# Retention on one core: weight sums by adding DMA transfers, sums of x kept in PSUM, scores between the third and the fourth quarter product

## What is computed

```python
def _retention(h, w_in, gn_g, w_out):            # h: normalised x, 512 x 1024
    proj = h @ w_in
    q, k, v, g = split(proj)                     # 4 heads, 256 wide for q and k, 512 for v and g
    q, k = _rope(q, pos), _rope(k, pos) * RET_DK ** -0.5
    ...                                          # over all chunks this is, per head:
    #   o[n] = sum over m of decay[n, m] * (q[n] . k[m]) * v[m]
    o = (o - mean(o)) * rsqrt(var(o) + EPS) * gn_g
    y = silu(g) * o
    return y @ w_out                             # added to x
```

## Time and profile before

| | us |
|---|---|
| median of 3 executions | 1906.8 (1903.63 to 1907.77) |
| the profiled execution, own time | 1903.31 |
| its span, first to last instruction | 1901.5 |
| busy in the span: PE, PEld | 1830.7 (96%), 1557.2 (82%) |
| busy in the span: DVE, POOL, ACT | 1262.2 (66%), 1018.6 (54%), 874.0 (46%) |

### The profile page before, as it was taken

The page is one execution under the profiler, slowest core; times in us unless marked ns, Lnnn a source line. Parts: engine busy times, 40 slices in busy tenths (PEclk is TensorE's granted clock), DMA queues, the critical chain, the costliest instruction groups (busy, mean ns, idle before and its releaser), DMA issues.

```text
span 1901.5 us, 23957 instructions
## 1 busy us (share of the span) xinstructions
PE 1830.7 (96%) x9348; PEld 1557.2 (82%) x9348; DVE 1262.2 (66%) x1908; ACT 874.0 (46%) x1350; POOL 1018.6 (54%) x431
## 2 busy tenths in 40 slices
PE   9999999999977999999899999999999999999998
PEld 7778889898865787878689898988888887888886
DVE  6986875776779667575766354457777766454546
ACT  5345443343543424243446444454666655453444
POOL 5573465475535365656438475665333335664755
PEclk9999999999997999999999999999999999999999
DMA  5222414423245325151342422312433223414221
GB/s 183 89 89 77 145 67 148 159 92 106 80 147 183 133 71 187 66 171 67 110 145 77 133 89 89 134 45 66 121 109 101 88 69 109 155 47 149 92 90 55
DMA packets 143344, 206.02 MB, mean 108 GB/s; under 512 B 4320, under 2 KB 94704, under 8 KB 142720
## 3 DMA queue, kind: packets, MB, share of 16 engines
q1 hardware_dynamic: 135968, 192.16, 30.2%
q10 hardware_dynamic: 7264, 12.34, 2.2%
HBM read 193.96 MB, written 10.53 MB: 108 GB/s over the span
## 4 chain that ended last, share of the span: by engine, by line
PE 72%; DVE 15%; ACT 4%; issue 3%; POOL 1%; DMA 0%; ACTq 0%; DVEq 0%
PE ps L858 23%; PE ps L860 23%; PE ps L859 23%; DVE ps L2315 1%; POOL w_lo L824 1%; ACT w_hi L1411 1%; DVE w_lo L2563 1%; DVE work L2611 1%; DVE raw L2549 1%; DVE diagonals L1983 1%; DVE work L2778 1%; DVE work L2574 0%; DVE probs_t_lo L2797 0%; PE ps L1198 0%; DVE x L2627 0%
## 5 line engine op out<-in xcount | busy, mean ns | idle before, releaser
L824 POOL TENSOR_TENSOR w_lo<-raw,w_hi 128x1024 fp32r<-128x1024 f32 x216 | 527.4, 2451 | 609.4 <-ACT w_hi L1411 609.4
L858 PE MATMUL ps<-xh,w_hi 128*128 128x512 f32 x1280 | 504.9, 394 | 4.6 <-DVE xl L2009 2.3
L860 PE MATMUL ps<-xh,w_lo 128*128 128x512 f32 x1280 | 498.9, 390 | 0.0
L859 PE MATMUL ps<-xl,w_hi 128*128 128x512 f32 x1280 | 498.8, 390 | 0.0
L1411 ACT ACTIVATE w_hi<-raw 128x1024 fp32r<-128x1024 f32 x242 | 252.2, 1057 | 392.9 <-PE ps L860 344.2
L858 PEld LDWEIGHTS ps<-xh,w_hi 128*128 128x128 f32 x1280 | 240.7, 188 | 58.5 <-issue 8.9
L859 PEld LDWEIGHTS ps<-xl,w_hi 128*128 128x128 f32 x1280 | 240.8, 188 | 50.7 <-issue 1.9
L860 PEld LDWEIGHTS ps<-xh,w_lo 128*128 128x128 f32 x1280 | 240.7, 188 | 50.7
L858 PE MATMUL ps<-hid,w_hi 128*128 128x256 f32 (+1 forms) x688 | 228.4, 332 | 2.1 <-DVE att_v L2751 1.1
L860 PE MATMUL ps<-hid,w_lo 128*128 128x256 f32 (+1 forms) x688 | 227.1, 330 | 0.0
L859 PE MATMUL ps<-hid,w_hi 128*128 128x256 f32 (+1 forms) x688 | 227.0, 330 | 0.0
(11 more groups left out here) (302 smaller groups left out, 3546.7 us busy)
## 6 DMA issues: line engine op xcount, KB each, us to landing
raw<-in_mlp_w_dram SPq DMA_DIRECT2D x40, 1024.0 KB, 5.5
work<-in_mlp_w_dram SPq DMA_DIRECT2D x16, 1024.0 KB, 5.5
raw<-in_ret_w_in_dram SPq DMA_DIRECT2D x12, 1024.0 KB, 5.2
raw<-in_att_w_in_dram SPq DMA_DIRECT2D x12, 1024.0 KB, 5.3
raw<-in_w_gate_dram SPq DMA_DIRECT2D x11, 1024.0 KB, 5.4
raw<-in_w_up_dram SPq DMA_DIRECT2D x11, 1024.0 KB, 5.5
hid<-position_sums SPq DMA_DIRECT2D x10, 1024.0 KB, 5.2
raw<-in_w_in_dram SPq DMA_DIRECT2D x9, 1024.0 KB, 5.1
```

Source lines behind the costliest of these rows:

```text
L824: nc.gpsimd.tensor_tensor(half_of(wl[:, b % 2, :], b, half), half_of(source, b, half), half_of(wh[:, b % 2, :], b, half).bitcast(F32), ALU ...
L858: nc.tensor.matmul(o, a[0], b[0], start=first, stop=False, skip_group_check=True)
L859: nc.tensor.matmul(o, a[0], b[1], start=False, stop=False, skip_group_check=True)
L860: return nc.tensor.matmul(o, a[1], b[0], start=False, stop=last, skip_group_check=True)
```

## The change

The signs of the seven products are changed so that each weight sum is one addition to a block already held: p1 = b12 + b11, p2 = p1 + b22, p3 = b22 + b12, p4 = p2 + b21. GpSimd issues each as a DMA transfer from DRAM that adds to the holder; no engine computes them, and the low halves of d2 and d4 go to GpSimd. The sums of x are formed in PSUM banks 6 and 7, in the order w (not stored), d2, d1, h22, d3; h22's stays in its place, so three are stored in place of four. `spread` moves behind h11, the scores of every head between h22 and d2, the mix of head 3 takes the order of the others. The normalising is folded into the gate: ScalarE scales the gate by the norm factor (`scale_gate`) and `gated` subtracts the mean and multiplies in one operation. The scaling of x (`scale_x`) moves to two later places of head 0. The core of the diff:

```diff
-BY_VECTOR = ("t2", "t4", "d2", "d4")
+BY_VECTOR = ("t2", "t4")
-        SUM_ROW = {"d1": 0, "d2": 1, "d3": 2, "h22": 3}
+        SUM_ROW = {"d1": 0, "d2": 1, "h22": 2, "d3": 3}
+        sum_rows = [o_sb[:, 2:4, :], ps[:, 6:8, :], o_sb[:, 0:2, :], ps[:, 6:8, :]]
+        root_guess = ps[:, 5, 0:ST]
+        sums_upto = {"w": 4, "d2": 8, "d1": 12, "h22": 16, "d3": 20}
...
 # SyncE
-                    fetch("b11", 0)
                     fetch("b12", 0)
+                    fetch("b22", 0)
...
                             converted("o0", h - 1)
-                            fetch("b22", h)
+                            fetch("b11", h)
                             converted("o1", h - 1)
                             fetch("b21", h)
+                        if more:
+                            converted("h11", h)
+                            fetch("q", h + 1)
                         multiplied("d1", h)
                         fetch_sum("d3")
                         if more:
-                            sp.wait_ge(d2_made, 2 * (h + 1))
-                            sp.wait_ge(d3_made, 2 * (h + 1))
-                            converted("h22", h)
-                            fetch("q", h + 1)
-                            multiplied("h22", h)
-                            fetch_sum("h22")
                             converted("d3", h)
                             fetch("k", h + 1)
...
 # GpSimd
+            def add_to(held, name, h, signal):
+                dst = holders[holder_of(held, h)].rearrange("p (k c) -> p k c", c=512)
+                nc.gpsimd.dma_start(dst, head_weights(name, h), accum_op=ALU.add).then_inc(signal, 16)
...
-                if kind == "h11":
-                    ...
-                        nc.gpsimd.tensor_tensor(first[:, cut], second[:, cut], first[:, cut], ALU.subtract).then_inc(d1_made, 1)
+                if kind == "own" and own_at[b][0] == "k":
+                    h = own_at[b][1]
+                    pool.wait_ge(*landed("b12", h))
+                    add_to("b12", "b11", h, p1_landed)
+                if kind == "d1":
+                    pool.wait_ge(w_lo, lows[2 * b + 2])
+                    add_to("b12", "b22", head_of(b), p2_landed)
                 if kind == "h22":
-                    ...
+                    pool.wait_ge(w_lo, lows[2 * b + 2])
+                    add_to("b22", "b12", head_of(b), p3_landed)
+                if kind == "d2":
+                    pool.wait_ge(w_lo, lows[2 * b + 2])
+                    add_to("b12", "b21", head_of(b), p4_landed)
...
 # TensorE
-                    spread()
                     for h in range(RET_HEADS):
                         head_quarter("h11", h)
+                        if h == 0:
+                            spread()
+                        head_quarter("d1", h)
+                        head_quarter("h22", h)
                         head_scores()
-                        for kind in ("d1", "h22", "d2", "d3"):
-                            head_quarter(kind, h)
+                        head_quarter("d2", h)
+                        head_quarter("d3", h)
                         pe.wait_ge(pt_ready, c.next(pt_ready, 4))
                         head_mix(h, (0, 1))
-                        if not more:
-                            head_mix(h, (2, 3))
                         head_quarter("h21", h)
-                        if more:
-                            head_mix(h, (2, 3))
+                        head_mix(h, (2, 3))
                         head_quarter("d4", h)
...
 # ScalarE
-                        act.wait_ge({"d1": d1_made, "d2": d2_made, "d3": d3_made, "d4": d4_made}[kind], 2 * h + half + 1)
+                        act.wait_ge({"d1": p1_landed, "d2": p2_landed, "d3": p3_landed, "d4": p4_landed}[kind], 16 * (h + 1))
...
+                    def scale_gate(h):
+                        act.wait_ge(root_refined, h + 2)
+                        for s in range(ST):
+                            act.wait_ge(gate_made, 4 * h + s + 1)
+                            nc.scalar.activation(sg[:, s, :], sg[:, s, :], ACT.Copy, scale=t4[:, s:s + 1]).then_inc(gate_scaled, c.made(gate_scaled))
...
                     def head(h, prepare=None):
+                        for _ in range(6):
+                            after_unit()
+                        scores_hi(range(ST))
                         after_unit()
                         after_unit()
-                        scores_hi((0, 1))
-                        after_unit()
-                        after_unit()
-                        scores_hi((2, 3))
-                        for _ in range(4):
-                            after_unit()
                         value_tile_hi(h, 0)
...
                         gate_curve(h, 2)
                         gate_curve(h, 3)
+                        scale_gate(h)
...
                     make_root()
+                    scale_far(4)
+                    position_sum_hi("d1")
+                    position_sum_hi("d2")
+                    qk_hi_of(qh)
+                    position_sum_hi("h22")
+                    act.wait_ge(sum_lo, SUM_ROW["d2"] + 1)
+                    scale_far(0)
+                    position_sum_hi("d3")
+                    make_root()
                     qk_hi_of(kh)
...
 # VectorE
-                        V.tensor_tensor(ms2, rc2, rc2, ALU.mult).then_inc(dve_step, c.made(dve_step))
+                        V.tensor_tensor(ms2, root_guess, ms, ALU.mult).then_inc(dve_step, c.made(dve_step))
...
+                        V.scalar_tensor_tensor(ms2, root_guess, -0.5, ms2, ALU.mult, ALU.mult).then_inc(dve_step, c.made(dve_step))
...
+                        V.scalar_tensor_tensor(rc2, ms2, 1.5, root_guess, ALU.add, ALU.mult).then_inc(root_refined, c.made(root_refined))
...
                     def gated(i):
-                        dve.wait_ge(gate_made, c.next(gate_made))
-                        dve.wait_ge(dve_step, c.now(dve_step))
-                        V.tensor_tensor(o_sb[:, i, :], o_sb[:, i, :], sg[:, i, :], ALU.mult).then_inc(p_ready, c.made(p_ready))
+                        dve.wait_ge(gate_scaled, c.next(gate_scaled))
+                        V.scalar_tensor_tensor(o_sb[:, i, :], o_sb[:, i, :], mv[:, i, 0:1], sg[:, i, :],
+                                               ALU.subtract, ALU.mult).then_inc(p_ready, c.made(p_ready))
...
                         keep_product(1, sg[:, 1, :])
-                        second_difference(h)
-                        score(h, 0)
-                        score(h, 1)
-                        score_lo(0)
                         keep_product(2, sg[:, 2, :])
                         keep_product(3, sg[:, 3, :])
-                        difference_lo("d2", h)
-                        ...
-                        fourth_difference(h)
+                        for j in range(ST):
+                            score(h, j)
+                        for j in range(ST):
+                            score_lo(j)
                         dve.wait_ge(pt_ready, c.now(pt_ready))
                         keep_product(2, third_added[0])
                         keep_product(3, third_added[1])
...
-                    position_sum(0)
-                    position_sum(1)
-                    position_sum_lo(0)
-                    position_sum_lo(1)
+                    for kind in ("w", "d2", "d1"):
+                        position_sum(kind)
+                    position_sum_lo("d1")
+                    position_sum_lo("d2")
                     rope(qh, ql, 0)
+                    position_sum("h22")
+                    position_sum_lo("h22")
+                    position_sum("d3")
+                    position_sum_lo("d3")
                     V.tensor_copy(ms, r1c).then_inc(to_curve, c.made(to_curve))
                     refine_root()
+                    dve.wait_ge(root_refined, c.now(root_refined))
                     diagonals(rc2, spread=False)
```

## The result

| | before | after |
|---|---|---|
| median, us | 1906.9 (1903.63 to 1907.77) | 1930.2 (1929.28 to 1932.34) |
| span of the profiled execution | 1901.5 | 1927.5 |
| mean granted clock of TensorE | 0.988 | 0.979 |

The ratio is 1.0127, with an interval of 1.0109 to 1.0145: slower by 23.3 us, where 7.3 us less was forecast. The prediction was wrong in sign, and the time lies 9 us above its range.

The account below looks back on a forecast made before the run. TensorE's waits, 48.2 us in six groups released by VectorE, were taken as the bound. Head 0 gains 9.3, heads 1 and 2 nothing, head 3 loses 2.0: together 7.3 off 1906.8 gives 1899.5 us, range 1880 to 1921.

Parts of the forecast that it names:

- The opening up to d1: Head 0's start: h11 at 562.6 instead of 572.04, TensorE waiting 9.1 us for the diagonals, d1's weights ready at 581.5.
- The transposes: TensorE's wait at each head's end: gone in heads 0 to 2, 8 to 9 us in head 3.
- the gate's term: Normalising moved into the gate: 1.9 us gained in each of heads 0 to 2, 1.1 lost in head 3.
- d3's stall: TensorE's third quarter product waits for value sum 0 behind the late third sum and score parts: 4.35 us every head.
- The prediction's own sign of being wrong: Adding transfers landing outside 7 to 11 us, or TensorE waiting at a place not named.
- y: Time from the end of the preceding low half to an adding transfer's landing: 9.2 us, bounds 5.2 and 13.8.
- rival 2: Third sum shares DMA engines with d3's fetched sum of x: y 10 to 12, 1903 to 1911; 0.19 with Rival 4.
- the turns between VectorE and GpSimd: Score low parts alternate with GpSimd's two low halves of d3; without turns the stall would be about 1 us.
- Rival 3: Third sum late at ScalarE's wait ahead of d3's conversion, 4 us per us of y, above 1911 us; chance 0.27.
- The prediction's slope: d3's stall falls by 1 us per us of y; the time moves by 4, since four heads pay.
- Rival 1: Adding transfer as quick as a plain one, y 5.2 to 7: 1882 to 1886 us; chance 0.22 (below 1894).
- Rival 4: Opening gains nothing: GpSimd's low halves hold VectorE twice more, head 0 gains 4.5, 1904 us; 0.19 with rival 2.

Follow-up runs that it names:

- Experiment 8: Kernel before, with only the gate scaled by the root on ScalarE and mean and gate in one VectorE instruction, all heads: 1898.6 us, ratio 0.9971.
- experiment 5: Changed kernel, with GpSimd's four transfers per head overwriting their block instead of adding to it: 1909.0 us, ratio 1.0028 to the kernel before.
- experiment 3: Changed kernel, with SyncE fetching d3's sum of x only when the third adding transfer has landed: 1923.3 us, ratio 1.010 to the kernel before.
- Experiment 2: Changed kernel, with decayed scores kept in PSUM, so VectorE's low parts read one SBUF and one PSUM tile: 1898.3 us, ratio 0.9975 to the kernel before.
- experiment 1: Changed kernel, with ScalarE making the scores' high parts before it waits for the third sum: 1885.0 us, ratio 0.9902 to the kernel before.
- experiment 6: Changed kernel, with the scores of heads 1 to 3 back behind h11 on all three engines, head 0 as changed: 1894.7 us, ratio 0.9951 to the kernel before.

## Why the prediction was wrong

**What it had right.** The waits it named are the waits there are, and nowhere else does TensorE stop for over 0.7 us. The opening up to d1: h11 was forecast at 562.6 and began at 562.37, the diagonals' product at 578.9 and 577.9, d1 at 581.5 and 580.3. The transposes: gone in three heads, 8.5 and 8.6 in the last. Experiment 8 confirms the gate's term to 0.1 us. The step to look at is d3's stall. The prediction's own sign of being wrong, landings outside 7 to 11 us, did not show: by groups they landed after 8.4 to 11.0. It was set on the transfer, and most of the miss lay in the queues behind it; the sign that did show it was d3's wait, 3 to 6 us by the prediction and 8.9 to 11.3 in the trace.

**The term that failed: 4.35 us in every head, measured 11.2 in heads 1 to 3.** Taken apart in head 1, from T:

| link | forecast | measured | off by |
|---|---|---|---|
| h22's low halves end | T+11.0 | 697.33 - 684.81 = 12.5 | 1.5 |
| y, to the landing | 9.2 | 708.71 - 697.33 = 11.4 | 2.2 |
| from there to the end of the low parts | 7.75 | 720.22 - 708.71 = 11.5 | 3.8 |
| copies and value sum, to d3's start | 1.95 | 722.34 - 720.22 = 2.1 | 0.2 |
| d3 wanted | T+25.55 | 711.19 - 684.81 = 26.4 | -0.8 |

The sum of the last column is 6.9: 4.35 + 6.9 = 11.2. In head 0 the third sum landed 9.0 us after the low half, as priced (599.50 - 590.51), and d3 still waited 8.85; the prediction's own path for this head gives 610.3 - 604.8 = 5.5 and not 4.35. There the third link of the table alone, 11.6 in place of 7.75, makes the miss.

*The 1.5* are GpSimd's issue of the second sum, which holds it for 1.29 us in front of h22's low halves. The prediction put 1.0 for an issue into y, and forgot the one that stands ahead of y. (It also took 2.4 for each of the four low halves; its row, 10.45 for four, would have given T+11.85.)

*The 2.2.* Alone, an adding transfer lands 8.4 to 8.6 us after its issue, 8.7 to 9.0 after the low half: the price taken (two passes and an issue, 9.2) was sound, and its second pass is near what experiment 5 measures, 2.4 to 3.0 us for the addition (3.0 was taken). What raised it to 11.4 was the fetch of d3's sum beside it, rival 2's mechanism; experiment 3 takes it out and has 8.6. The prediction argued the fetch away because it is issued first. It is, and the third sum was 2.4 us longer beside it all the same.

*The 3.8.* The prediction saw the turns between VectorE and GpSimd, and let VectorE's first part wait for one of GpSimd's low halves and the other three for one more. It did not look at what GpSimd would have queued by then: ScalarE, held up by the late sum, converts h21 right behind d3 (712.06), so four low halves stand ready and four parts of VectorE alternate with them. The 1.52 of rows 8 was the sign of it: one low part, one turn; four low parts are four turns, as long as GpSimd has four operations to take turns with. The Trainium skill (SBUF — State Buffer, § Who interferes with whom) says that a VectorE instruction with two SBUF inputs and a GpSimd one that reads SBUF exclude each other. Experiment 2 agrees: 2300 ns for one part, 485 with one operand in PSUM.

**A price left out: the clock.** The prediction read in the earlier trace rows that products behind a long wait run slow, up to 1.8 us, and charged this to the opening alone. Its own stall of 4.35 us in each of four heads got none. In the changed kernel the product behind the stall takes 8.36 us in place of 5.6, so 2.8 us a head. Head 1 then closes: h11 to h11 took 99.29 before and 108.70 after, 9.4 more; by the waits 11.15 - 4.3 = 6.9, by the clock 2.8, together 9.7, 0.3 too much.

**Over the heads.** By head 1's h11 (688.30 before, 684.81 now) 3.5 us were gained in place of 9.3 (head 0's d3 wait is 8.9, and the product behind it slow), heads 1 and 2 lost 9.4 and 9.7 in place of nothing, and what follows, head 3 mainly, lost 10.4 in place of 2.0.

**The rivals.** Rival 3 had the right place, ScalarE's wait ahead of d3's conversion, with the right things queued behind it, and 1930 for a y of 16.8. It came to 1930 with a y of 11.4: the place was right, and that the time agrees is luck, since y was not the largest part. The prediction's slope, 1 us of wait for each us of y, held in heads 1 to 3: in experiment 5 y falls from 11.4 to 9.0 in head 1 and the wait from 11.15 to 8.75, and in experiment 2 the 2.4 us of the third sum come off the waits of heads 2 and 3. That the span falls by more than this in experiment 5 comes mostly from head 0: its wait is 7.45 shorter, and d3 behind it takes 5.6 us and no longer 8.2 from start to start. Rival 1 falls with experiment 5 as far as the addition goes. Rival 4's gain of 4.5 for head 0 is near the 3.5 measured, but not for its reason: the opening came as forecast up to d1, and d3's stall took the rest.

**What the sum lacked as a whole** was to ask whether the stall belonged to the change at all. It does not: experiment 1 keeps the transfers, the sums and the late scores, and gives 1885, 1.0 per cent below the kernel before. The last score was ready at 705.9 in head 1, and ScalarE got to the first at 710.62.

**What stays open.** How much of the 9 us that experiment 6 gains comes from the transfers and how much from the opening was not separated; only the gate's 4.6 was. Nor was the fetch of d3's sum tried at an earlier place, since its slot is free only when d1 is multiplied.

## What to carry to other kernels

When a step is moved behind a wait on an in-order engine, list what stands behind that wait and could have gone ahead of it; here, exchanging two entries of ScalarE's list was worth 43 us. Where two engines take turns at a resource, count the instructions that both will have queued at that moment, not those of the one chain under study; and where an operand can lie in PSUM instead, the turns go away. Charge each wait of several us with the slow product behind it, wherever the wait stands.

## What was not expected of the hardware

- An adding transfer of 1 MB from GpSimd's queue took 8.4 to 8.5 us from issue to landing and 11.0 beside another 1 MB (medians); the same transfer without the addition 5.6 to 6.1, and 8.0. Its issue held GpSimd for 1.29 us, without the addition for 0.77.
- With two operands in SBUF, four small VectorE instructions took 8.96 us beside four queued GpSimd instructions, 4.68 beside two, and 1.69 alone: VectorE waited a whole GpSimd instruction for each of its own.
- A wait of 11 us put the 5.6 us product behind it to 8.36 us, and the granted clock of its 80 us stretch was 0.91 where it had been 1.00.
